# A hybrid attention and MLP block in fp32: gate sums spread over four up-projection units, and unused products on TensorE in three waits at the turn to the MLP

## The chip, the core and the metric

The kernel runs on one core of one Trainium2 chip. The metric is the device time of one execution in microseconds. A program on one core has one span; the median of several executions is compared.

## What is computed

One encoder block on 512 tokens of width 2048, in fp32. Two attention groups share an input projection and an output projection; their result is gated and added to x. Then comes the MLP, which is where the change lies:

```python
mod = c_act @ w_ada[l] + b_ada[l]
sh_a, sc_a, gt_a, sh_m, sc_m, gt_m = [m[:, None, :] for m in jnp.split(mod, N_MOD, axis=-1)]
...
o = o @ w_out[l]
x = x + gt_a * rms_norm(o, g_post_attn[l])

h = rms_norm(x, g_pre_mlp[l]) * (1.0 + sc_m) + sh_m
y = jnp.square(jax.nn.relu(h @ w_mlp_in[l])) @ w_mlp_out[l]
x = x + gt_m * rms_norm(y, g_post_mlp[l])
```

The hidden width is 8192. The gate of the MLP, gt_m, is a product of the activated vector c with 2048 columns of w_ada; it is wanted only at the very end, multiplied by g_post_mlp.

## The kernel before

Every engine has its own program, and they meet at semaphores. A matrix product in fp32 is done as three products of split values: an operand is split into a high part (`hi`, rounded, by ScalarE) and a low part (`lo`, the rest, by VectorE), and TensorE multiplies high by high, high by low and low by high, 128 x 128 weights against 512 columns each time.

**The turn to the MLP.** The last block of the output projection is done token tile by token tile (L2444 to L2446), so that VectorE can start on tile 0 early: it adds and gates a tile (L1739, L1744), adds it to x (L1790), and ScalarE sums squares and scales (L1104, L1087). The last of the four tiles is scaled by VectorE itself (L1810), for lack of time on ScalarE. TensorE, behind its last output product, waits for the last tile sum (`b_sum`), then turns the first 512 columns of each scaled tile, four transposes a tile, into banks 4 to 7 (L2462 to L2470), waiting for each tile (`xn_ready`). ScalarE and VectorE read the turned banks, scale and shift them (L1114, L1115, L1816), and split them into `h2_hi` and `h2_lo` (L1118, L1821). `first_columns` (L2474 on) is TensorE's first MLP unit, taken apart so that it can start with `h2_hi` of one row block alone (L2481, L2482: eight products), then take its `h2_lo` (L2485), then the second row block (L2489 to L2491). Bank 0 is free at the turn until L2481 writes it. `o_hi` is the high part of the old attention output; it lies where `h2_hi` will be written.

**The up-projection.** The MLP has eight groups of 1024 hidden columns. Each has two halves of eight units; a unit is 24 products (`unit_columns`, L2082 to L2084). The halves use banks 0 to 3 and 4 to 7 in turn. ScalarE and VectorE square the relu of a finished half, split it, mix it for the fast down product, and GpSimd stores it to DRAM (`y_dram`, L2698): a store waits for the one before it. Weights pass through a ring of four raw slots that SP fills.

**The gate.** Over groups 0 to 6, VectorE multiplies rows of w_ada by c and adds them up in `gm_acc` (L1262, L1265), 128 partial sums a column. In the last group TensorE adds the partitions: a product with a matrix of ones for each 512 columns (L2549), all four ahead of unit 6 of the first half, into banks 4 to 7, which the second half will use from unit 8 on. One count of `gm_reduced` is given by the last of them. ScalarE waits for it behind its work for unit 9 (L1168) and copies the four banks back into `gm_acc` (L1170), counting `gm_copied`. TensorE waits for four of these before unit 8 (L2553). GpSimd waits for four as well (L2714), then does four rounds in series: load 512 entries of b_ada and of g_post_mlp, spread to all partitions, into `rows` (L2711, L2712), add the one and multiply by the other (L2716, L2717). Then it gives `comb_m_ready`, and goes on to the four stores of the last group's activation.

**The down products.** SP, behind its last up loads, waits for `comb_m_ready`, because y values 1 lie where `rows` was, then issues the load of y values 1 and of weight blocks 22 and 21 for the first half of columns; behind TensorE's last up product the y values 2, 3 and 4; behind VectorE's last `y_ready` y values 6; behind all stores y values 5 and the blocks 11, 12 and 22 of the second half of columns. VectorE's down group (`dn_group`) begins with the difference of blocks 22 and 12 (L1893), then low halves (L1889) and further differences in a fixed order, with the last relu work of the up phase between them, and it takes finished banks away (L1963). TensorE's down unit is 12 products (L2519 to L2521); 14 such units make one half of columns.

The queue on each engine is fixed by the order in which the program is written. SP's loads, in short:

```python
sp.wait_ge(comb_m_ready, 1)
values(0, 1)
for k, (blk, h) in enumerate((("22", 0), ("22", 1), ("21", 0), ("21", 1))):
    sp.wait_ge(raw_used, MLP_RAW_END - RING + k + 1)
    weights(0, 0, blk, (h,))
sp.wait_ge(w_used, DN_W)
for k in (2, 3, 4):
    values(0, k)
sp.wait_ge(y_ready, GROUPS * PAIRS)
values(0, 6)
sp.wait_ge(y_saved, 16 * GROUPS * PAIRS)
values(0, 5)
weights(0, 1, "11")
```

Of the kernel before, what the change touches and what calls it, by code (L numbers as in the profile page):

```python
# [26 lines left out]
P = 128  # L27
T = 512
NT = T // P
D = 2048  # L30
KD = D // P
COLS = 512
NB = D // COLS
# [7 lines left out]
GROUPS = 8  # L41
FCH = D_FF // GROUPS // P
# [7 lines left out]
UNITS_D = KD // QROWS  # L50
# [143 lines left out]
def build(nc, a, out, x1_dram, y_dram):  # L194
    with ExitStack() as ctx:
# [22 lines left out]
        ones = small("ones", [P])  # L218
# [72 lines left out]
        gm_acc = sb("gm_acc", 180, [D])  # L291
# [426 lines left out]
        def _(act):  # L718
# [436 lines left out]
            def mlp_group(g, first=False, last=False):  # L1155
                for j in range(FIRST_SPLIT if first else 0, MLP_N):
                    r, w = at_mlp(g, j)
                    split_hi(r, w)
                    if 3 <= j < 6 and not first:
                        if j == 3:  # L1160
                            act.wait_ge(w_used, w.count(1, 1 - 4))
                        after_up(g - 1, 1, j - 3)
                    if UNITS_D + 3 <= j < UNITS_D + 6:
                        if j == UNITS_D + 3:
                            act.wait_ge(w_used, w.count(1, 1 - 4))
                        after_up(g, 0, j - UNITS_D - 3)
                    if last and j == UNITS_D + 1:
                        act.wait_ge(gm_reduced, 1)  # L1168
                        for n in range(NB):
                            nc.scalar.activation(gm_acc[:, n * COLS:(n + 1) * COLS], sets[1][n][:], ACT.Copy).then_inc(gm_copied, 1)  # L1170

# [883 lines left out]
        def _(pe):  # L2055
            mm = nc.tensor.matmul

            def unit_tokens(w, acc, act_hi, act_lo, k0, first, last, tiles=None, only=range(NT), behind_first=None):

                s = w.slot()  # L2060
                for t in only:
                    if t and tiles:
                        ins.then_inc(tiles, 1)
                    if t == 1 and behind_first:
                        behind_first()
                    for q in range(QROWS):
                        k = k0 + q
                        xh, xl = act_hi[:, k, t * P:(t + 1) * P], act_lo[:, k, t * P:(t + 1) * P]
                        mm(acc[t][:], xh, hi[s][:, q, :], start=first and q == 0, stop=False)  # L2069
                        mm(acc[t][:], xh, lo[s][:, q, :], start=False, stop=False)  # L2070
                        ins = mm(acc[t][:], xl, hi[s][:, q, :], start=False, stop=last and q == QROWS - 1)  # L2071
                if t == NT - 1:
                    ins.then_inc(w_used, 1)
# [387 lines left out]
            def turn_x1(k, t, out_bank):  # L2461
                return nc.tensor.transpose(out_bank[:, t * P:(t + 1) * P], z_tok[:, t, k * P:(k + 1) * P], ident[:])  # L2462

            pe.wait_ge(b_sum, 4 * NB)
            for t in range(NT):
                pe.wait_ge(xn_ready, t + 1)
                for k in range(4):
                    ins = turn_x1(k, t, bank[4 + k])
                    if t == NT - 1:
                        ins.then_inc(xn_turned, 1)  # L2470
            pe.wait_ge(row_done, 4 * NB)


# [69 lines left out]

            def spread_gm(j):

                if j == UNITS_D - 2:
                    pe.wait_ge(y_done, (GROUPS - 1) * FCH)
                    for n in range(NB):
                        ins = mm(sets[1][n][:], ones[:], gm_acc[:, n * COLS:(n + 1) * COLS], start=True, stop=True)  # L2549
                    ins.then_inc(gm_reduced, 1)  # L2550

            up_block(GROUPS - 1, 0, spread_gm)
            pe.wait_ge(gm_copied, NB)  # L2553
# [206 lines left out]
```

## Time and profile before

| | us |
|---|---|
| three runs | 2116.38, 2115.14, 2108.70 |
| their median | 2115.14 |
| the profiled execution, its own time | 2110.3 |
| its span, first to last instruction | 2108.6 |
| TensorE matmul busy | 2058.1 |
| VectorE busy | 1498.1 |
| ScalarE busy | 843.6 |
| GpSimd busy | 154.6 |
| mean granted TensorE clock | 0.993 |

The times of single instructions come from the profiled execution, in microseconds from its first instruction. Its span leaves out 1.7 us that its own time has around it. PE is TensorE, DVE VectorE, ACT ScalarE, POOL GpSimd, SP the engine that issues most transfers; L12 is line 12 of the kernel. Products overlap in their pipeline: the duration of one (0.39 us) is longer than the pitch from one to the next.

### The profile page before, as it was taken

What the parts mean: (1) busy time and instruction counts of PE and PEld (TensorE: products, weight loads), DVE (VectorE), ACT (ScalarE), POOL (GpSimd) and SP (SyncE); (2) the same over time, 40 slices, a digit from 0 to 9 for tenths busy, and PEclk for the clock granted to TensorE, in tenths of its full rate; (3) what the DMA queues carried; (4) which work ended last, traced back from release to release, by engine and by line L of the source; (5) the groups of instructions that cost most, each with busy time, mean ns of one, the idle gap of its engine ahead of it and who ended that gap; (6) DMA issues with size and microseconds to landing.
All of it is one profiled execution on the core that took longest, in us unless ns stands there. A gap on an engine that the chain in (4) does not pass through costs nothing.

```text
span 2108.6 us, 26190 instructions
## 1 busy us (share of the span) xinstructions
PE 2058.1 (98%) x9314; PEld 1701.0 (81%) x9314; DVE 1498.1 (71%) x1804; ACT 843.6 (40%) x1153; POOL 154.6 (7%) x163
## 2 busy tenths in 40 slices
PE   6999999999999989999999999999999999999998
PEld 6888888878888778888888888888788888888886
DVE  5986898788877766455444554435889888888866
ACT  4454223588833364233223333333333433333322
POOL 0000000157500000000000000012000000000000
PEclk9999999999999999999999999999999999999999
DMA  9997768600377637656665566676757356456442
GB/s 312 335 310 232 256 208 244 200 20 11 110 262 246 231 139 253 196 181 219 229 200 187 189 216 231 199 239 225 252 222 269 136 212 250 159 199 239 179 180 80
DMA packets 214353, 435.20 MB, mean 206 GB/s; under 512 B 30180, under 2 KB 69768, under 8 KB 205448
## 3 DMA queue, kind: packets, MB, share of 16 engines
q1 hardware_dynamic: 196136, 361.43, 51.0%
q0 software_dynamic: 16704, 67.11, 9.0%
q10 hardware_dynamic: 1440, 5.70, 0.7%
q8 instruction: 44, 0.72, 0.1%
q14 instruction: 29, 0.24, 0.0%
HBM read 367.09 MB, written 67.11 MB: 206 GB/s over the span
## 4 chain that ended last, share of the span: by engine, by line
PE 83%; DVE 6%; DMA 4%; ACT 3%; issue 3%; SPq 0%; DVEq 0%; ACTq 0%; POOLq 0%
PE bank L2082 11%; PE bank L2084 11%; PE bank L2083 11%; PE bank L2519 7%; PE bank L2520 7%; PE bank L2521 7%; PE bank L2069 5%; PE bank L2071 5%; PE bank L2070 5%; PE bank L2570 1%; PE bank L2569 1%; PE bank L2568 1%; DMA raw<-in_w_ada 1%; PE bank L2140 1%; DMA w<-in_w_mlp_out 1%
## 5 line engine op out<-in xcount | busy, mean ns | idle before, releaser
L1238 DVE TENSOR_TENSOR lo<-raw,hi 128x1024 fp32r<-128x1024 f32 (+2 forms) x234 | 276.4, 1185 | 373.7 <-ACT hi L725 371.5
L725 ACT ACTIVATE hi<-raw 128x1024 fp32r<-128x1024 f32 (+2 forms) x236 | 239.7, 1023 | 654.6 <-PE bank L2084 410.4
L2082 PE MATMUL bank<-h_hi,hi 128*128 128x512 f32 x1016 | 396.0, 390 | 0.0
L2084 PE MATMUL bank<-h_hi,lo 128*128 128x512 f32 x1016 | 395.3, 389 | 0.0
L2083 PE MATMUL bank<-h_lo,hi 128*128 128x512 f32 x1016 | 395.2, 389 | 0.0
L2519 PE MATMUL bank<-hi,y_use 128*128 128x512 f32 x784 | 307.7, 392 | 7.8 <-DVE acc L1965 3.8
L2520 PE MATMUL bank<-lo,y_use 128*128 128x512 f32 x784 | 306.1, 390 | 0.0
L2521 PE MATMUL bank<-hi,y_use 128*128 128x512 f32 x784 | 306.1, 390 | 0.0
L1181 ACT ACTIVATE hi<-w 128x1024 fp32r<-128x1024 f32 x168 | 178.3, 1062 | 296.8 <-PE bank L2521 218.3
L1889 DVE TENSOR_TENSOR lo<-w,hi 128x1024 fp32r<-128x1024 f32 x168 | 204.1, 1219 | 37.3 <-ACT hi L1181 36.2
L2082 PEld LDWEIGHTS bank<-h_hi,hi 128*128 128x128 f32 x1016 | 190.8, 188 | 40.0 <-issue 0.6
L2084 PEld LDWEIGHTS bank<-h_hi,lo 128*128 128x128 f32 x1016 | 190.7, 188 | 39.7
L2083 PEld LDWEIGHTS bank<-h_lo,hi 128*128 128x128 f32 x1016 | 190.8, 188 | 39.5 <-issue 0.2
L2519 PEld LDWEIGHTS bank<-hi,y_use 128*128 128x128 f32 x784 | 147.8, 189 | 43.6 <-issue 13.2
L2521 PEld LDWEIGHTS bank<-hi,y_use 128*128 128x128 f32 x784 | 147.8, 189 | 31.0
L2520 PEld LDWEIGHTS bank<-lo,y_use 128*128 128x128 f32 x784 | 147.9, 189 | 30.4
L2069 PE MATMUL bank<-hi,h_hi 128*128 128x512 f32 x320 | 125.9, 394 | 1.4 <-ACT q_o L883 1.4
L2071 PE MATMUL bank<-hi,h_lo 128*128 128x512 f32 x320 | 124.7, 390 | 0.0
L2070 PE MATMUL bank<-lo,h_hi 128*128 128x512 f32 x320 | 124.5, 389 | 0.0
L1965 DVE TENSOR_TENSOR acc<-bank,acc 128x1024 f32<-128x1024 f32 x84 | 102.1, 1216 | 0.0
L2069 PE MATMUL bank<-hi,o_hi 128*128 128x512 f32 x224 | 88.7, 396 | 0.1
L2071 PE MATMUL bank<-hi,o_lo 128*128 128x512 f32 x224 | 87.3, 390 | 0.0
(326 smaller groups left out, 3111.6 us busy)
## 6 DMA issues: line engine op xcount, KB each, us to landing
raw<-in_w_ada SPq DMA_DIRECT2D x192, 512.0 KB, 5.1
raw<-in_w_mlp_in SPq DMA_DIRECT2D x128, 512.0 KB, 4.3
w<-in_w_mlp_out SPq DMA_DIRECT2D x128, 512.0 KB, 5.2
y_dram<-y_out POOLq DMA_DIRECT2D x32, 1792.0 KB, 8.7
y_use<-y_dram SPq DMA_DIRECT2D x53, 1024.0 KB, 8.8
raw<-in_w_in SPq DMA_DIRECT2D x32, 512.0 KB, 5.6
raw<-in_w_out SPq DMA_DIRECT2D x32, 512.0 KB, 5.0
raw<-in_w_in SPq DMA_DIRECT2D x48, 256.0 KB, 5.5
```

The source lines that it names most:

```text
L725: ins = nc.scalar.activation(dst, src, ACT.Copy)
L1238: ins = tt(dst, src, high.bitcast(F32), ALU.subtract)
L1889: tt(lo[w.slot()][:], weight(np, i, h)[:], hi[w.slot()][:].bitcast(F32), ALU.subtract).then_inc(dn_lo, 1)
L2069: mm(acc[t][:], xh, hi[s][:, q, :], start=first and q == 0, stop=False)
L2070: mm(acc[t][:], xh, lo[s][:, q, :], start=False, stop=False)
L2071: ins = mm(acc[t][:], xl, hi[s][:, q, :], start=False, stop=last and q == QROWS - 1)
L2082: mm(acc[n][:], wh, act_hi[:, k, :], start=first and q == 0, stop=False)
L2083: mm(acc[n][:], wh, act_lo[:, k, :], start=False, stop=False)
L2084: ins = mm(acc[n][:], wl, act_hi[:, k, :], start=False, stop=last and q == QROWS - 1)
L2519: mm(bank[b + m][:], yh, hi[s][:, q, :], start=j == 0, stop=False)
L2520: mm(bank[b + m][:], yh, lo[s][:, q, :], start=False, stop=False)
L2521: ins = mm(bank[b + m][:], yl, hi[s][:, q, :], start=False, stop=j == PAIRS - 1)
```

## The change

Five places on TensorE, one on ScalarE. `gm_reduced` is now counted once per sum, so ScalarE waits for four.

```diff
@@ ScalarE, behind its work for unit 9 of the last group
-                        act.wait_ge(gm_reduced, 1)
+                        act.wait_ge(gm_reduced, NB)
                         for n in range(NB):
                             nc.scalar.activation(gm_acc[:, n * COLS:(n + 1) * COLS], sets[1][n][:], ACT.Copy).then_inc(gm_copied, 1)
@@ TensorE
             mm = nc.tensor.matmul
+
+            def keep_busy(n, out_bank, held, moving):
+
+                for _ in range(n):
+                    mm(out_bank, held, moving, start=True, stop=True)
@@ the turn to the MLP
+            keep_busy(4, bank[0][:], o_hi[:, KD - 1, 0:P], o_hi[:, KD - 1, :])
             pe.wait_ge(b_sum, 4 * NB)
             for t in range(NT):
+                if t == NT - 1:
+                    keep_busy(17, bank[0][:], o_hi[:, KD - 1, 0:P], o_hi[:, KD - 1, :])
                 pe.wait_ge(xn_ready, t + 1)
                 for k in range(4):
                     ins = turn_x1(k, t, bank[4 + k])
                     if t == NT - 1:
                         ins.then_inc(xn_turned, 1)
+            keep_busy(4, bank[0][:], o_hi[:, KD - 1, 0:P], o_hi[:, KD - 1, :])
             pe.wait_ge(row_done, 4 * NB)
@@ the last group, first half
             def spread_gm(j):
 
-                if j == UNITS_D - 2:
-                    pe.wait_ge(y_done, (GROUPS - 1) * FCH)
-                    for n in range(NB):
-                        ins = mm(sets[1][n][:], ones[:], gm_acc[:, n * COLS:(n + 1) * COLS], start=True, stop=True)
-                    ins.then_inc(gm_reduced, 1)
+                if j >= UNITS_D - NB:
+                    n = j - (UNITS_D - NB)
+                    pe.wait_ge(y_done, (GROUPS - 1) * FCH - NB + n + 1)
+                    mm(sets[1][n][:], ones[:], gm_acc[:, n * COLS:(n + 1) * COLS], start=True, stop=True).then_inc(gm_reduced, 1)
 
             up_block(GROUPS - 1, 0, spread_gm)
```

The 25 products of `keep_busy` multiply a part of the old `o_hi` with itself into bank 0; nothing reads what they write. UNITS_D is 8 and NB is 4, so the gate sums stand ahead of units 4, 5, 6 and 7.

## Rows read from the trace of the kernel before

**Rows 1.** The page, part 1: busy us, share of the span, instructions.
```profile
PE 2058.1 (98%) x9314; PEld 1701.0 (81%) x9314; DVE 1498.1 (71%) x1804; ACT 843.6 (40%) x1153; POOL 154.6 (7%) x163
```
**Rows 2.** TensorE's waits: line, releaser, us in total, times, longest.
```profile
PE bank L2462 <- DVE z_tok L1810: 3.9, 1, 3.9
```
**Rows 3.** Timeline of the turn: start us, us, engine, line, instruction [idle before <-releaser].
```profile
748.12 0.39 PE L2446 MATMUL bank<-hi,o_lo 128*128 128x512 f32 x1
...
749.56 1.06 PE L2462 MATMUL bank<-ident,z_tok 128*128 128x128 f32 x8 [1.05 <-DVE part L1739]
...
751.52 0.66 PE L2462 MATMUL bank<-ident,z_tok 128*128 128x128 f32 x4 [0.91 <-ACT z_tok L1087]
...
755.55 1.41 DVE L1810 TENSOR_SCALAR z_tok<-x_res,rstd 128x512 f32<-128x512 f32 x2
...
756.10 1.12 PE L2462 MATMUL bank<-ident,z_tok 128*128 128x128 f32 x4 [3.92 <-DVE z_tok L1810]
756.70 0.76 ACT L1114 ACTIVATE h_f<-bank,shf_m,gsc_m 128x512 f32<-128x512 f32 x1
...
758.15 1.29 DVE L1821 TENSOR_TENSOR h_lo<-h_f,h_hi 128x512 fp32r<-128x512 f32 x2 [0.47 <-ACT h_hi L1115]
...
758.27 0.77 PE L2481 MATMUL bank<-h_hi,hi 128*128 128x512 f32 x1 [1.05 <-ACT h_hi L1115]
...
761.50 1.09 PE L2485 MATMUL bank<-h_lo,hi 128*128 128x512 f32 x4
...
762.42 0.39 PE L2489 MATMUL bank<-h_hi,hi 128*128 128x512 f32 x1
```
**Rows 4.** TensorE in a stretch of the turn: stretch, length, busy, granted clock, DMA.
```profile
754.00:754.50 0.50, 0.00 (x0) 0.76 0.51 213
```
**Rows 5.** Timeline of the gate sums, TensorE and ScalarE.
```profile
1407.11 3.59 PE L2549 MATMUL bank<-gm_acc,ones 128*128 128x512 f32 x8
...
1410.74 2.07 ACT L1170 ACTIVATE gm_acc<-bank 128x512 f32<-128x512 f32 x4 [2.32 <-PE bank L2549]
1410.77 0.40 PE L2083 MATMUL bank<-h_lo,hi 128*128 128x512 f32 x1
```
**Rows 6.** Timeline of GpSimd's gate rounds: first add, a slow multiply, the last multiply.
```profile
1413.51 1.28 POOL L2716 TENSOR_TENSOR gm_acc<-gm_acc,rows 128x512 f32<-128x512 f32 x1 [10.47 <-DMA rows<-in_g_post_mlp]
...
1424.02 2.17 POOL L2717 TENSOR_TENSOR gm_acc<-gm_acc,rows 128x512 f32<-128x512 f32 x1
...
1443.58 1.30 POOL L2717 TENSOR_TENSOR gm_acc<-gm_acc,rows 128x512 f32<-128x512 f32 x1
```
**Rows 7.** SP from 1380 to 1530: a row of its waits, one of its timeline.
```profile
SPq L611 <- POOLq L2718: 19.5, 1, 19.5
...
1445.33 2.46 SPq L604 DMA_DIRECT2D w<-in_w_mlp_out  x4
```
**Rows 8.** Timeline of the first down units: VectorE, and TensorE's units 0 and 6.
```profile
1458.32 1.23 DVE L1893 TENSOR_TENSOR diff<-w,w 128x1024 f32<-128x1024 f32 x1 [12.36 <-DMA w<-in_w_mlp_out]
...
1478.32 2.35 DVE L1889 TENSOR_TENSOR lo<-w,hi 128x1024 fp32r<-128x1024 f32 x2
...
1464.95 0.39 PE L2519 MATMUL bank<-hi,y_use 128*128 128x512 f32 x1
...
1481.27 0.39 PE L2519 MATMUL bank<-hi,y_use 128*128 128x512 f32 x1
```
**Rows 9.** Timeline: GpSimd's stores 2 to 4, SP's next weights, TensorE's second wait.
```profile
1460.55 0.96 POOL L2698 DMA_DIRECT2D y_dram<-y_out  x1 [13.97 <-DMA y_dram<-y_out]
1473.74 0.94 POOL L2698 DMA_DIRECT2D y_dram<-y_out  x1 [12.23 <-DVE y_out L1852]
1481.89 0.94 POOL L2698 DMA_DIRECT2D y_dram<-y_out  x1 [7.21 <-DMA y_dram<-y_out]
...
1489.38 34.69 SPq L604 DMA_DIRECT2D w<-in_w_mlp_out  x14
...
1506.12 0.76 PE L2519 MATMUL bank<-hi,y_use 128*128 128x512 f32 x1 [2.92 <-DVE lo L1889]
```

## The prediction

> **What bounds the kernel now.** The page first: TensorE's matmuls fill 98% of the span [rows 1]. A change that adds or removes nothing large on TensorE can only act through the few stretches in which TensorE waits. The list of TensorE's waits names 3.9 us at the turn to the MLP, for the last normalised tile [rows 2]; in it stands also one of 2.9 us in the first group of down products, for a low half of a weight, whose own row is in rows 9. The timeline of the turn [rows 3] and the clock there [rows 4] price the first edit. For the second I followed the gate sums from TensorE to ScalarE's copies [rows 5], to GpSimd [rows 6], to the SP queue [rows 7], to VectorE's first down work [rows 8] and to the second wait [rows 9].
>
> **The products at the turn (25 added).** After its last output product, begun at 748.12 and streaming until about 748.35, TensorE waits until 749.56 for VectorE's tile, turns two tiles, waits 0.91 us, turns tile 2 (751.52, 0.66 us), waits 3.92 us and turns tile 3 at 756.10; then it waits for the first h2_hi until 758.27 [rows 3]. The granted clock (2.4 GHz) is full until about 754.2 (a mean of 0.76 over 754.0 to 754.5) [rows 4] and then half. At full clock products follow at 0.23 us ((762.42 - 761.50) / 4), at half clock at 0.40 ((761.50 - 758.27) / 8, the last of them already faster) [rows 3].
>
> - Four products ahead of the b_sum wait take 4 x 0.23 = 0.92 us, from 748.35 to 749.27. The wait ends at 749.56: cost nothing, hidden by 0.3 us of it.
> - Seventeen products behind the third tile's turn take 17 x 0.23 = 3.9 us from about 752.0 (751.52 plus four turns at some 0.11 us): they end at about 755.9, and tile 3 is ready at 756.1. Cost nothing, but the cover left is 0.2 us. From above: if the clock falls at 754.2 all the same, some 7 products still to come run at about 0.40 instead of 0.23 and the turn comes 1.0 us late. From below: nothing is gained by the products themselves.
> - Four products behind the fourth tile's turn, about 756.6 to 757.5, fit ahead of the first h2_hi.
>
> What they buy: with the clock held, the turn of a tile takes 0.66 instead of 1.12 us, and ScalarE, which starts 0.60 us behind the first of the half-clock turns [rows 3], starts about 0.3 us earlier; so does the first MLP product. The eight products from 758.27 to 761.50 take 8 x 0.23 = 1.84 instead of 3.23 us. The h2_lo tiles that the next products want are written by 759.44 [rows 3], so no new wait takes over at once. Together 0.3 + 1.4 = 1.7 us gained (bounds: 1.0 lost, 1.7 gained). I take the gain: the clock survived waits of 1.05 and 0.91 us here, fell only two microseconds into the long one [rows 3, 4], and the products leave no gap longer than the first two. All later MLP work is released by TensorE or behind it, so the gain should carry on.
>
> **The gate sums, on TensorE.** The eight passes (two per sum) run from 1407.11; the product that would have been at 1407.34 comes at 1410.77: 3.43 us for four sums, or 0.86 each [rows 5]. One ahead of each of units 4 to 7 costs the same 3.43 us. The bank waits are spread too, but VectorE released those banks long before unit 4. Cost: nothing; gain: nothing.
>
> **The gate sums, for those who wait.** Here the change has a price. ScalarE copies all four sums only when the count is 4 (before: 1, set by the last sum). It did so at 1410.74, done at 1412.81 [rows 5]. Now the last sum stands ahead of unit 7, that is one unit later, a unit being 24 products, 24 x 0.227 = 5.44 us (0.227 is (1481.27 - 1464.95) / 72 down products of the same shape [rows 8]). TensorE has by then done the same sums, so the copies start at 1410.74 + 5.44 = 1416.2 and end at 1418.25. Behind them on ScalarE stands the high half of unit 10, some 2 us late, wanted by TensorE 14 us later: hidden. TensorE itself wants the copies at unit 8 (about 1421.4): hidden.
>
> GpSimd is not hidden. Its first gate product started at 1413.51, released by the landing of its rows [rows 6], so 0.7 us of the delay is absorbed, and it now starts at about 1418.35: **4.85 us later**. Behind it are four rounds in series (two row loads, an add, a multiply), each released by the round before: 1413.51 to 1444.88. The whole series moves by 4.85 us. At its end SP waits: the row SPq L611 <- POOLq L2718 gives 19.5 us, and only then come the loads of y values 1 and of weights 22 and 21 [rows 7]. GpSimd's own next work, the four stores of the last activation, is behind the series as well; the third waits for VectorE and the fourth for the third [rows 9].
>
> VectorE was idle for 12.36 us until 1458.32, when weights 22 landed, and then works almost without a gap [rows 8]. It moves to about 1463.2. TensorE enters the down products at 1464.95 and takes a unit of 12 products in 2.72 us, so unit 6 is due at 1464.95 + 6 x 2.72 = 1481.27; its low half is done at 1478.32 + 1.2 = 1479.5 [rows 8]. The cover is 1.8 us, the smallest of the first units (unit 0, whose low half is done two instructions behind 1458.32, has 4.2), so TensorE first loses 4.85 - 1.8 = 3.05 us, in small waits. The 14 units after these hang on the stores: VectorE's y_out, store 3 (1473.74), store 4 when it has landed (1481.89), SP's loads behind store 4 (1489.38), weights 22 for the next half, VectorE, TensorE at 1506.12 after its 2.92 us wait [rows 9]. Every link is released by the one before, so TensorE resumes 4.85 us later than it did. The 3.05 us are part of that, not added to it. Nothing behind gives it back, TensorE being 98% busy.
>
> Bounds of this term: from below 0, if weights 22 did not really wait for their issue but for traffic that ends at a fixed time; from above 4.85 plus the slow form of GpSimd's multiply. In two of four rounds the multiply took 2.17 instead of 1.30 us [rows 6], when VectorE was reading; two more such rounds would give 6.6. I take 4.85, as all rows of the chain show release by the link before.
>
> The Trainium skill (GPSIMD Engine Reference, 8. Key points) says that GpSimd shares its SBUF interfaces with VectorE and contends with VectorE instructions that have two SBUF inputs. The trace's two multiply times agree with that. By the rule alone the moved rounds 2 and 3 meet VectorE again as before and round 4 not, which leaves 4.85; were all four to meet it, the term would be 6.6.
>
> **The sum.** -1.7 + 0 + 4.85 = **+3.1 us**. The profiled execution took 2110.3 us, so its like would take 2113.4; the median of the three runs shown is 2115.14, 4.8 above it, and 2115.1 + 3.1 = **2118.2 us**, which I forecast. What a measurement of this kernel can tell from no change is about 0.5%, 10.6 us: this is no change.
>
> **The rivals.**
> - *The gate chain is hidden.* The landing of weights 22 would be set by bandwidth (they took 13.0 us from 1445.33 to 1458.32 [rows 7, 8]), and later transfers with less beside them would catch up. Against it: SP's wait for GpSimd is plain. Then only the turn counts: 2115.1 - 1.7 = 2113.4. Chance 0.17.
> - *The clock falls at the turn all the same*, or the seventeen overrun: +1.0 instead of -1.7, with the gate chain +5.9: 2121.0. This is also the case in which the products do not do what they are for. Chance 0.12.
> - *Slower by over 0.5%: the stores pile up.* Store 2 would now start at about 1465.4, in the moment in which TensorE's end of the up phase releases three loads of y values. Stores are in series: each waits for the one before, and SP's loads for the last. Stores 3 and 4 took 8.2 and 7.5 us from issue to the next link (1473.74, 1481.89, 1489.38); the first held GpSimd for 14 us beside SP's loads [rows 9]. If 2, 3 and 4 each take 13, the last lands at 1465.4 + 39 = 1504.4 instead of 1489.4: +15.0, less 1.7, is +13.3: 2128.4. It decides once the three together take over 36 us (1465.4 + 36.3 is 12.3 late). Against it: GpSimd waited before store 3 for VectorE's y_out, not for store 2 [rows 9], so store 2 had room, and the added overlap is short. Chance 0.06.
> - *Faster by over 0.5%*: no row offers 10.6 us; only the scatter of the runs does. Chance 0.03.
>
> **How the numbers follow.** Forecast 0.62. The first three cases stay within 0.5%: 0.62 + 0.17 + 0.12 = 0.91 same, 0.06 slower, 0.03 faster. The range takes the runs' own scatter (2108.7 to 2116.4) with the terms: down to 2108.7 - 1.7 = 2107, up to 2116.4 + 6.6 + 1.0, and 2 for the start of the pile-up, 2126. It leaves out most of the slower case.
>
> **What would show it right or wrong.** In the changed profile: a clock of 1.00 from 748 to 764, ScalarE's first h_f some 0.3 us and the L2489 products about 1.7 us earlier against the last output product; four single gate sums with 0.86 us each; ScalarE's copies 5.4 us and SP's load behind GpSimd 4.9 us later against the start of unit 4; TensorE waits of about 3 us in all in the first half of the down products and a wait of about 4.7 in place of 2.9 at the second. If VectorE's first down work is not later by some 5 us, the gate term falls; if the clock still halves near 754, the turn term does. A second half-clock stretch in the first down products would break the claim that the small waits cost only themselves.

## The result, and the profile after

The changed kernel takes 2117.74 us (median of 12 runs, 2115.76 to 2126.38), the kernel before 2113.41 (12 runs, 2107.11 to 2116.38) in the same measurement. The medians are 4.3 us apart, the means (2118.50 and 2112.04) 6.5 us; the ratio over all runs is 1.003, with a 95% interval of 1.002 to 1.004, some 4 to 8 us. The slowdown is real, since 1.000 lies outside the interval, and smaller than the 0.5% under which the prediction speaks of no change. The profiled execution took 2115.81 us with a span of 2114.1, against 2110.3 and 2108.6 before: +5.5.

The page and the list of TensorE's waits (line, releaser, us in total, times, longest) of the changed kernel. The 25 products are there (9339 matmuls for 9314 in [rows 1]), and the busy time is 6.4 us more.

```profile
span 2114.1 us, 26240 instructions
...
PE 2064.5 (98%) x9339; PEld 1705.0 (81%) x9339; DVE 1498.7 (71%) x1804; ACT 843.5 (40%) x1153; POOL 154.1 (7%) x163
...
PE bank L2528 <- DVE lo L1889: 8.1, 4, 6.2
```

The last row is the one to look at: the wait of 2.9 us in the down products [rows 9] has become 8.1 us in four pieces, the longest 6.2.

The turn to the MLP, timeline of the changed kernel (L2467 was L2462, L2494 was L2485):

```profile
749.32 0.39 PE L2451 MATMUL bank<-hi,o_lo 128*128 128x512 f32 x1
...
752.72 0.66 PE L2467 MATMUL bank<-ident,z_tok 128*128 128x128 f32 x4 [1.08 <-ACT z_tok L1087]
753.13 4.13 PE L2061 MATMUL bank<-o_hi 128*128 128x512 f32 x17
...
757.31 0.66 PE L2467 MATMUL bank<-ident,z_tok 128*128 128x128 f32 x4
...
757.91 0.76 ACT L1114 ACTIVATE h_f<-bank,shf_m,gsc_m 128x512 f32<-128x512 f32 x1
...
759.48 0.47 PE L2490 MATMUL bank<-h_hi,hi 128*128 128x512 f32 x1 [0.58 <-ACT h_hi L1115]
...
761.39 1.07 PE L2494 MATMUL bank<-h_lo,hi 128*128 128x512 f32 x4
```

Stretches of the changed kernel (stretch, length, PE busy, granted clock, DMA share, GB/s), and under them one of the kernel before:

```profile
754.00:756.00 2.00, 2.00 (x11) 1.00 0.26 111
...
758.00:760.00 2.00, 1.42 (x6) 1.00 0.81 269
```
```profile
756.00:758.00 2.00, 1.12 (x4) 0.50 0.91 259
```

The clock is 1.00 (2.4 GHz) in every stretch of 2 us from 748 to 762; before it was 0.50 (1.2 GHz) from 756 to 760. The eight products that follow the first h_hi take 761.39 - 759.48 = 1.91 us, 3.23 before [rows 3]. ScalarE starts 0.60 us behind the last tile's turn, as before, although the turn now runs at full clock.

The gate chain, rows from the timelines of ScalarE, GpSimd, SP, VectorE and TensorE in the changed kernel:

```profile
1416.19 2.07 ACT L1170 ACTIVATE gm_acc<-bank 128x512 f32<-128x512 f32 x4 [6.09 <-PE bank L2558]
...
1418.41 1.29 POOL L2724 TENSOR_TENSOR gm_acc<-gm_acc,rows 128x512 f32<-128x512 f32 x1 [14.48 <-ACT gm_acc L1170]
...
1447.33 1.29 POOL L2725 TENSOR_TENSOR gm_acc<-gm_acc,rows 128x512 f32<-128x512 f32 x1
...
1449.08 2.50 SPq L604 DMA_DIRECT2D w<-in_w_mlp_out  x4
...
1463.17 1.22 DVE L1893 TENSOR_TENSOR diff<-w,w 128x1024 f32<-128x1024 f32 x1 [17.36 <-DMA w<-in_w_mlp_out]
...
1464.34 0.95 POOL L2706 DMA_DIRECT2D y_dram<-y_out  x1 [14.03 <-DMA y_dram<-y_out]
...
1479.70 0.94 POOL L2706 DMA_DIRECT2D y_dram<-y_out  x1 [14.41 <-DMA y_dram<-y_out]
...
1480.80 0.50 PE L2528 MATMUL bank<-hi,y_use 128*128 128x512 f32 x1 [0.59 <-DVE lo L1889]
...
1484.53 0.47 PE L2528 MATMUL bank<-hi,y_use 128*128 128x512 f32 x1 [0.72 <-DVE lo L1889]
...
1487.98 0.94 POOL L2706 DMA_DIRECT2D y_dram<-y_out  x1 [7.33 <-DMA y_dram<-y_out]
...
1496.20 33.98 SPq L604 DMA_DIRECT2D w<-in_w_mlp_out  x13
...
1512.78 0.77 PE L2528 MATMUL bank<-hi,y_use 128*128 128x512 f32 x1 [6.23 <-DVE lo L1889]
```

Read two releasers. GpSimd's first add is now released by ScalarE's copies, before by the landing of its rows [rows 6]. And store 3 (1479.70) is released by the landing of store 2; before it was VectorE's y_out [rows 9]. VectorE's y_out was itself 5.0 us later, counted from the turn (1477.61 against 1472.75), and store 2 held store 3 for another 1.1 us. The chain that ended last (start, us) shows how: stores 1 and 2 are on it whole, and store 2 takes twice what stores 3 and 4 take. It runs beside three loads of y values; before the change it had landed after 8.1 us.

```profile
1449.33 14.42 DMA y_dram<-y_out
...
1464.34 14.81 DMA y_dram<-y_out
...
1479.70 7.72 DMA y_dram<-y_out
1487.98 7.83 DMA y_dram<-y_out
```

**Where the time went.** Executions differ ahead of the change too: the last output product starts anywhere from 746.8 to 757.5 us in the profiles of this study. So I cut each profiled execution at three marks. A "turn" is one 128 x 128 transpose, and the first group of 16 turns of the MLP starts at 765.16 before and at 765.02 after. "Start" is the start of the last output product, A goes from it to the first group of 16 turns of the MLP, B from there to the end of TensorE's wait for the second half's first low half (of weights 22; 1506.12 before, 1512.78 after), C is the rest of the span. All in us.

| kernel | start | A | B | C |
|---|---|---|---|---|
| before | 748.12 | 17.04 | 740.96 | 602.48 |
| changed | 749.32 | 15.70 | 747.76 | 601.32 |
| turn_only | 748.19 | 15.70 | 739.99 | 601.32 |
| spread_only | 747.97 | 17.59 | 749.87 | 601.87 |
| one_earlier | 751.00 | 15.67 | 741.95 | 601.38 |
| weights_ahead | 749.55 | 15.73 | 749.87 | 602.25 |
| store_between | 757.52 | 15.72 | 751.83 | 601.43 |
| both_orders | 749.46 | 15.69 | 744.23 | 601.62 |
| both_and_earlier | 753.61 | 15.72 | 741.55 | 601.42 |
| seventeen_only | 749.69 | 15.68 | 749.43 | 601.70 |
| thirtyfour | 746.84 | 19.09 | 749.04 | 601.43 |
| eight_only | 747.21 | 16.25 | 748.65 | 601.59 |

The two kernels whose name begins with loads_ahead are not in the table, because their wait stands at another product. B and C together are 1350.03 for loads_ahead_changed and 1342.98 for loads_ahead_turn, against 1349.08 changed, 1341.31 turn_only and 1343.44 before.

Changed less before: +1.20 ahead of the change, -1.34 at the turn, +6.80 up to the second wait's end, -1.16 after it. The last three, which are the change's own, make +4.30; the medians say +4.33. That these agree so closely is luck: each column rests on one execution, and for spread_only and turn_only the same sum gives +8.85 and -3.47 where the medians say +7.0 and -4.4. Nor is the low clock at the turn a constant price: spread_only, with nothing changed at the turn, has an A that is 0.55 longer than before, so what the products save there is 1.3 to 1.9 us.

The -1.16 is clock: it is complete 36 products behind the wait, which are reached after 11.03 us before and after 9.88 in the changed kernel. Stretches around the second wait, before and then changed:

```profile
1504.00:1506.00 2.00, 0.00 (x0) 0.80 1.05 386
...
1512.00:1514.00 2.00, 2.00 (x10) 0.99 0.00 0
```
```profile
1508.00:1510.00 2.00, 0.00 (x0) 0.84 1.05 394
...
1516.00:1518.00 2.00, 2.00 (x10) 0.95 0.00 0
```

A mean of 0.80 over 2 us is 0.8 us at 0.50, so before the clock fell at about 1505.2; it was back at about 1512.0, after 6.8 us. By the same reading of the changed kernel it fell at about 1509.4 and was back at about 1516.2: 6.8 us too. But before only 0.9 us of them lay in the wait and 5.9 over products, and in the changed kernel 3.4 lay in the wait and 3.4 over products. A product takes 0.43 us at half clock and 0.227 at full, so 0.47 of such time is lost: 2.8 us before, 1.6 now, a difference of 1.2. The longer wait swallowed half of the low clock. Where the fall comes within a wait is no property of the change, so this part may differ from execution to execution: it came 2.0 us behind the start of the wait before, 2.8 us in the changed kernel and 4.8 us in one_earlier.

The marks of the gate chain, each counted from the first group of 16 turns, so that A and what lies ahead drop out:

| mark | before | changed | spread_only | one_earlier |
|---|---|---|---|---|
| GpSimd's first add | 648.35 | 653.39 | 653.46 | 648.28 |
| SP's loads of weights 22 | 680.17 | 684.06 | 685.78 | 679.60 |
| VectorE's first down work | 693.16 | 698.15 | 698.55 | 692.43 |
| store 2 | 695.39 | 699.32 | 701.04 | 694.80 |
| store 3 | 708.58 | 714.68 | 716.68 | 707.86 |
| SP's weights, second half | 724.22 | 731.18 | 733.32 | 725.45 |
| TensorE, end of second wait | 740.96 | 747.76 | 749.87 | 741.95 |

### The profile page after: what moved, and what is told of

It reads as the page before. It is cut to its first block, busy times and chain, and to the rows that moved or that the text cites. A ratio compares the mean times of both kernels' runs of the same rounds, so it can differ in the third digit from the quotient of the medians.

```text
span 2114.1 us, 26240 instructions
## 1 busy us (share of the span) xinstructions
PE 2064.5 (98%) x9339; PEld 1705.0 (81%) x9339; DVE 1498.7 (71%) x1804; ACT 843.5 (40%) x1153; POOL 154.1 (7%) x163
## 4 chain that ended last, share of the span: by engine, by line
PE 84%; DVE 5%; DMA 4%; issue 3%; ACT 3%; POOL 1%; SPq 0%; DVEq 0%; ACTq 0%; POOLq 0%
PE bank L2089 10%; PE bank L2087 10%; PE bank L2088 10%; PE bank L2528 7%; PE bank L2530 7%; PE bank L2529 7%; PE bank L2074 6%; PE bank L2076 6%; PE bank L2075 6%; DMA y_dram<-y_out 2%; PE bank L2578 1%; PE bank L2577 1%; PE bank L2576 1%; PE bank L2145 1%; PE bank L2146 1%
```

## The experiments

**First group: the parts alone, the place of the last sum, and SP's order.** The kernel before took 2112.49 us here (35 runs). The changed kernel was not measured again, here or in the two other groups; ratios are to the kernel before of the same group.

turn_only: the changed kernel with the gate sums and ScalarE's count as before.

```diff
-                        act.wait_ge(gm_reduced, NB)
+                        act.wait_ge(gm_reduced, 1)
@@ spread_gm
-                if j >= UNITS_D - NB:
-                    n = j - (UNITS_D - NB)
-                    pe.wait_ge(y_done, (GROUPS - 1) * FCH - NB + n + 1)
...
+                if j == UNITS_D - 2:
+                    pe.wait_ge(y_done, (GROUPS - 1) * FCH)
...
```

> The 25 products at the turn alone; the gate sums as before (four ahead of unit 6, one count). My theory: the clock stays full from 748 to 764, the eight L2490/L2491 products take 1.9 instead of 3.2 us, and nothing else moves: 1.3 to 1.7 us faster than the kernel before, and about 5 to 6 us faster than the changed one. Rival (the products overrun or buy nothing): 0 to 1 us slower than before.

Measured 2108.08 us (2106.19 to 2112.0), ratio 0.9981 (0.9969 to 0.9994): 4.4 us faster than before, where 1.3 to 1.7 had been expected. A is 1.34 shorter, B 0.97 and C 1.16. Timeline of the second wait:

```profile
1503.88 0.47 PE L2528 MATMUL bank<-hi,y_use 128*128 128x512 f32 x1 [1.95 <-DVE lo L1889]
```

The product behind the wait takes 0.47 us, not 0.76 as in [rows 9], and the granted clock is 1.00 in every stretch of 2 us from 1500 to 1522. What the 25 products do directly is A. B is a shorter second wait, 1.95 for 2.92 us, and C the half clock that did not come, 2.8 us, less a further wait of 1.09 us at 1510.69; that would be 1.7, and the 0.5 between it and 1.16 are not explained. The GpSimd multiplies took 1.28 to 1.30 us here, where two took 2.17 and 2.16 before [rows 6], but one add took 1.97 instead of 1.28. A single execution doesn't show that the turn causes this.

spread_only: the changed kernel without `keep_busy` and its three calls.

```diff
-            keep_busy(4, bank[0][:], o_hi[:, KD - 1, 0:P], o_hi[:, KD - 1, :])
-                    keep_busy(17, bank[0][:], o_hi[:, KD - 1, 0:P], o_hi[:, KD - 1, :])
-            keep_busy(4, bank[0][:], o_hi[:, KD - 1, 0:P], o_hi[:, KD - 1, :])
```

> The gate sums ahead of units 4 to 7 alone, ScalarE waiting for four; no products at the turn. My theory: GpSimd's first add starts about 4.9 us later, released by ScalarE's copy and no longer by its rows; TensorE's second down wait grows from 2.9 to 6 or 7 us; 5 to 7 us slower than before. Rival (the down phase is set by bandwidth, the gate chain hidden): within 0.5 us of before.

Measured 2119.45 us (2113.36 to 2125.65), ratio 1.0031 (1.0017 to 1.0045): +7.0. The two parts together are -4.4 + 7.0 = +2.6 by medians, where the whole change gave +4.3; the intervals of both parts reach some 3 us to either side, so they add up within what is measured. The expectation (5 to 7 us, a second wait of 6 or 7) held: 7.0, and 6.23. The delay stands in its column of the second table: 5.1 at the first add, 8.1 at store 3, 8.9 at TensorE.

one_earlier: the four single sums ahead of units 3, 4, 5 and 6, so that the last stands where all four stood before.

```diff
-                if j >= UNITS_D - NB:
-                    n = j - (UNITS_D - NB)
+                if UNITS_D - NB - 1 <= j < UNITS_D - 1:
+                    n = j - (UNITS_D - NB - 1)
```

> The changed kernel with the four gate sums ahead of units 3 to 6 in place of 4 to 7: still one per unit, but the last is where the four stood before. My theory (the price is the place of the last sum, not the spreading): GpSimd's first add goes back to being released by its rows, the second down wait back to about 2.9 us, and the time to that of turn_only, 5 us or so below the changed kernel. Rival (a lone fp32 sum between fp32r products costs TensorE or the clock something each time): it stays with the changed kernel.

Measured 2110.53 us (2107.09 to 2114.56), ratio 0.9989 (0.9976 to 1.0001). GpSimd's first add is again released by its rows:

```profile
1414.95 1.28 POOL L2724 TENSOR_TENSOR gm_acc<-gm_acc,rows 128x512 f32<-128x512 f32 x1 [9.19 <-DMA rows<-in_g_post_mlp]
```

All marks of its column are within 1.3 us of before. So the price hangs on the place of the last sum: one unit earlier it is gone. The expectation held only in part, though. The time was to be that of turn_only and is 2.45 us above it by medians (1.9 by means, 95% interval about 0.3 to 3.6), and the second wait is not back at 2.9:

```profile
1508.62 0.47 PE L2528 MATMUL bank<-hi,y_use 128*128 128x512 f32 x1 [3.73 <-DVE lo L1889]
```

A small cost of spreading as such, up to some 3 us, is therefore not ruled out.

weights_ahead: on SP, the loads of weights 22 and 21 ahead of the wait for the gate chain. If SP's wait is what carries the price, this takes it away.

```diff
-            sp.wait_ge(comb_m_ready, 1)
-            values(0, 1)
             for k, (blk, h) in enumerate((("22", 0), ("22", 1), ("21", 0), ("21", 1))):
...
+            sp.wait_ge(comb_m_ready, 1)
+            values(0, 1)
```

> The changed kernel with one order turned round on SP: the loads of weights 22 and 21 stand ahead of the wait for GpSimd's gate rounds, only y values 1 behind it. My theory (VectorE's late start hangs on that wait, the second TensorE wait on the stores behind the gate rounds): VectorE's first down difference no longer waits until 1463, the three small TensorE waits go, the stores have fewer loads beside them and take 8 instead of 15 us, and the second wait shrinks to under 3 us or goes: 7 to 10 us faster than the changed kernel, 3 to 5 faster than before. Rival (bandwidth decides, the bytes being the same): within 2 us of the changed kernel.

Measured 2117.58 us (2112.85 to 2122.86), ratio 1.002 (1.0006 to 1.0034). My expectation missed: VectorE no longer waits 17 us for its weights, and nothing is gained. Timeline of store 3 and of TensorE's last wait:

```profile
1480.97 0.94 POOL L2706 DMA_DIRECT2D y_dram<-y_out  x1 [14.76 <-DMA y_dram<-y_out]
...
1515.15 0.77 PE L2528 MATMUL bank<-hi,y_use 128*128 128x512 f32 x1 [6.13 <-DVE lo L1889]
```

Store 2 takes 15 us again and holds store 3. The prediction had two ways from GpSimd to the second wait, over SP and VectorE to y_out, and over the stores. This run cuts the first: y_out comes 1.1 us earlier than before, counted from the turn (1471.79 - 765.28 = 706.51, against 707.59), and store 3 still comes 7.1 us later. So the stores can carry the whole price alone. It does not show what the first way costs alone, and the edit has a price of its own: the weights now run beside the gate rounds, which end 3.4 us later than in the changed kernel (1450.99 - 765.28 = 685.71 against 682.31), and store 1 starts 4.3 us later.

**Second group: the stores' order.** Before: 2111.28 us (23 runs).

store_between: GpSimd issues the first store between gate rounds 2 and 3 instead of behind round 4.

```diff
+                if n == 1:
+                    save_pair(GROUPS - 1, 0, 0)
             pool.sem_inc(comb_m_ready, 1)
-            save_group(GROUPS - 1)
+            save_pair(GROUPS - 1, 0, 1)
+            save_pair(GROUPS - 1, 1, 0)
+            save_pair(GROUPS - 1, 1, 1)
```

> The changed kernel with one order turned round on GpSimd: the first store of the last activation (ready at 1430) stands between the second and the third gate round, not behind the fourth. SP's order is as in the changed kernel. My theory as the first four runs leave it (the second down wait hangs on the four stores in series behind the gate rounds; VectorE's late start costs only the small waits): stores 1 and 2 land some 10 us earlier, store 3 is again released by VectorE's y_out, the second wait falls from 6.2 to 3 to 5 us (VectorE being late still), the small first waits stay or grow to 2 to 3 us as SP's wait ends 1 to 2 us later; 1 to 3 us faster than the changed kernel. Rival (the landing of SP's own loads sets the second wait, not the stores): no change against the changed kernel.

Measured 2123.71 us (2120.2 to 2128.25, 6 runs), ratio 1.0057 (1.0038 to 1.0076): a miss, and the slowest of all. The store slows the row loads of round 3: the wait ahead of its add is 8.89 us, 3.66 in the changed kernel (round 4: 4.14 and 4.28). With the issue of the store and slower adds and multiplies, SP's wait ends 7.3 us later than in the changed kernel and VectorE gets its weights 4.5 us later, both counted from the turn. VectorE's row:

```profile
1475.84 1.22 DVE L1893 TENSOR_TENSOR diff<-w,w 128x1024 f32<-128x1024 f32 x1 [21.08 <-DMA w<-in_w_mlp_out]
```

TensorE waits 5.01 and 5.49 us, and behind both the first product takes 0.77 us, which is half clock. A store in the middle is paid by the rounds behind it.

both_orders: SP's order of weights_ahead and GpSimd's of store_between together.

```diff
@@ SP
-            sp.wait_ge(comb_m_ready, 1)
-            values(0, 1)
...
+            sp.wait_ge(comb_m_ready, 1)
+            values(0, 1)
@@ GpSimd
+                if n == 1:
+                    save_pair(GROUPS - 1, 0, 0)
```

> The changed kernel with both orders turned round: SP's weights 22 and 21 ahead of its wait for the gate rounds, and GpSimd's first store between rounds two and three. My theory: each alone leaves the other path in place; together nothing of the last stretch hangs on the gate rounds. VectorE's y_out for store 3 is then set by the end of the up products (1465), store 4 lands near 1486, and the second wait falls to between 0 and 2 us with no half clock: 2103 to 2107, 10 to 14 us below the changed kernel and 6 to 9 below before. Rival (bandwidth from 1440 to 1510 decides): the second wait stays at 5 us or more.

Measured 2112.75 us (2110.35 to 2118.69), ratio 1.0005 (0.9991 to 1.0019). Some 5 us better than the changed kernel in its own measurement, and as before, but the expectation of 2103 to 2107 missed and its rival, a second wait of 5 us or more, came. No small waits are left in the first down products, and store 3 stands at the place of before (1473.82 - 765.15 = 708.67 from the turn), but it is released by store 2, store 4 comes 11.8 us behind it (8.2 before), and the second wait is 6.03 us.

both_and_earlier: the same, with the sums at units 3 to 6.

```diff
@@ on top of both_orders
-                if j >= UNITS_D - NB:
+                if UNITS_D - NB - 1 <= j < UNITS_D - 1:
...
```

> As both_orders, and the gate sums ahead of units 3 to 6. My theory: with the gate rounds off the path, the place of the last sum no longer counts: within 1.5 us of both_orders. Rival (the place of the last sum has a price of its own on TensorE or ScalarE): 3 us or more faster than both_orders.

Measured 2109.46 us (2106.94 to 2113.97), ratio 0.999 (0.998 to 1.0001), the same as one_earlier. Against both_orders it is 3.3 us faster by medians (3.1 by means, 95% interval about 1 to 5), so the expectation of "within 1.5 us" missed: even with both orders turned round the place of the last sum still counts. The profiles say how: in both_orders the rounds end 2.6 us later (692.82 against 690.18 from the turn), store 2 starts 3.5 us later and takes 12.4 us, and store 3 waits for it. Timelines:

```profile
1476.81 0.96 POOL L2706 DMA_DIRECT2D y_dram<-y_out  x1 [14.32 <-DVE y_out L1852]
...
1510.88 0.47 PE L2528 MATMUL bank<-hi,y_use 128*128 128x512 f32 x1 [3.32 <-DVE lo L1889]
```

Here neither the stores nor the weights are late, and the second wait is still 3.3 us. What is left is a series that starts with the last up product: VectorE's y_out (7 us), stores 3 and 4 (8.3 and 9.4 us to the next link), SP's loads (some 14 to VectorE) and the low half (2.5), some 41 us, beside fourteen units of 2.72, 38.1 us. It comes out between some 40 us (turn_only, a wait of 1.95) and 42 us (one_earlier, 3.73), so about 2 to 4 us of wait are left, and in no run did an earlier end of the gate rounds bring it below 1.95.

seventeen_only: the changed kernel without the two calls with four products.

```diff
@@ ahead of the wait for b_sum
-            keep_busy(4, bank[0][:], o_hi[:, KD - 1, 0:P], o_hi[:, KD - 1, :])
@@ behind the fourth tile's turn
-            keep_busy(4, bank[0][:], o_hi[:, KD - 1, 0:P], o_hi[:, KD - 1, :])
```

> The changed kernel with the seventeen products alone, the two fours left out. Read at the turn alone: if the seventeen hold the clock by themselves, it is 1.00 from 748 to 766 and the first L2494 comes 12.1 us after the last output product as in the changed kernel (before: 13.4). If the fours are wanted too, the clock falls somewhere between 754 and 762.

One run, 2118.23 us, read at the turn only. The clock is 1.00 in every stretch of 2 us from 748 to 764, and A is 15.68 against 15.70: the seventeen alone hold the clock, and beside them the eight others buy nothing.

**Third group: the loads behind the stores, and the number of products.** Before: 2112.0 us (23 runs).

loads_ahead_changed: SP loads blocks 12 and 22 of the second half ahead of its wait for the stores; y values 5 and block 11 stay behind it. The first turn of SP's loop is written out for this.

```diff
-            sp.wait_ge(y_saved, 16 * GROUPS * PAIRS)
-            values(0, 5)
-            weights(0, 1, "11")
@@ dn_loads
                 weights(*to, "22", free=free(8))
+                if first:
+                    sp.wait_ge(y_saved, 16 * GROUPS * PAIRS)
+                    values(0, 5)
+                    weights(0, 1, "11")
```

> The changed kernel, but SP issues the blocks 12 and 22 of the second half of columns ahead of its wait for the stores, with only y values 5 and block 11 behind it (the loop's first turn is written out for that). My theory (four stores in series behind the gate rounds, then SP's 4 MB of loads, then VectorE, set the second down wait): VectorE's second down difference no longer comes 14 us behind the last store, the second wait of 6.2 us falls to 0 to 2, perhaps with a wait of 1 to 3 us for y values 5 instead; the small first waits stay. 4 to 7 us below the changed kernel. Rival (VectorE or bandwidth alone sets it): no change, or later stores.

Measured 2117.0 us (2114.23 to 2122.45), ratio 1.0029 (1.0016 to 1.0042). The expectation (4 to 7 us below the changed kernel) missed, and its rival, no change, came. The wait of 6.23 us for the low half is gone, and a wait for y values 5 is in its place. Timeline of that wait, and store 4 from the chain that ended last:

```profile
1504.70 0.79 PE L2531 MATMUL bank<-hi,y_use 128*128 128x512 f32 x1 [5.01 <-DMA y_use<-y_dram]
...
1486.77 13.04 DMA y_dram<-y_out
```

Store 4 takes 13.0 us instead of 7.8, because the weights now run beside it. The bytes are the same, and the DMA share in the changed kernel is 1.0 and more from 1504 to 1514 (1.05 at 394 GB/s in the row of 1508 above), so the order of the loads moves the wait and shortens it by 1.2 us, from 6.23 to 5.01. That gains nothing: from the turn to the end of the span this profile is 0.95 us longer than the changed kernel's.

loads_ahead_turn: the same edit on turn_only.

```diff
@@ on top of turn_only, SP's dn_loads
                 weights(*to, "22", free=free(8))
+                if first:
+                    sp.wait_ge(y_saved, 16 * GROUPS * PAIRS)
...
```

> The same SP order on turn_only (the 25 products, gate sums as before the change). If the last leg behind the stores is the floor under which no earlier gate round could bring the second wait, this is the kernel that goes below it: the wait of 2 to 3 us goes, and with it the half clock that sometimes follows: 2 to 5 us below turn_only, 5 to 8 below before. Rival: the loads collide with stores 3 and 4 and give the gain back: the time of turn_only.

Measured 2109.46 us (2104.59 to 2112.24), ratio 0.9987 (0.9975 to 0.9998), not told apart from turn_only: the rival again, where 2 to 5 us had been expected. The wait is 2.53 us, for y values 5 once more, and half clock follows it (0.58 over 1500 to 1502).

thirtyfour: 34 products in the middle call instead of 17.

```diff
-                    keep_busy(17, bank[0][:], o_hi[:, KD - 1, 0:P], o_hi[:, KD - 1, :])
+                    keep_busy(34, bank[0][:], o_hi[:, KD - 1, 0:P], o_hi[:, KD - 1, :])
```

> The changed kernel with 34 products in place of 17 behind the third tile's turn. Read at the turn: they end at 753.1 + 34 x 0.23 = 760.9 on the changed kernel's clock instead of 757.0, the last tile's turn comes 3.6 us late, and so do h_f and the first L2494, all at full clock. If the products yielded to work that becomes ready, there would be no delay.

One run, 2118.1 us. A is 19.09, 3.39 more than with 17. Timeline:

```profile
750.66 7.98 PE L2061 MATMUL bank<-o_hi 128*128 128x512 f32 x34
...
758.48 0.60 PE L2467 MATMUL bank<-ident,z_tok 128*128 128x128 f32 x4
```

The tile is turned only when the last product is through. It stands 11.64 us behind the last output product instead of 7.99, as expected. Once the cover is used up, each product too many costs its own 0.23 us.

eight_only: the seventeen out, the two calls with four kept.

```diff
-                if t == NT - 1:
-                    keep_busy(17, bank[0][:], o_hi[:, KD - 1, 0:P], o_hi[:, KD - 1, :])
```

> The changed kernel with the two fours and without the seventeen. Read at the turn: if the seventeen are what holds the clock, it falls to half near 754 to 756 after the last output product's time of 749 and the first L2494 comes 13.1 to 13.4 us behind the last output product, as before the change (12.07 with all 25); if the fours suffice, 12.1.

One run, 2115.35 us. A is 16.25, between 15.70 and the 17.04 of before, and the first L2492 (L2494 in the changed kernel) comes 12.62 us behind the last output product: neither the 13.1 to 13.4 nor the 12.1 that were expected. Timeline of the last turn, and the clock:

```profile
755.18 1.12 PE L2467 MATMUL bank<-ident,z_tok 128*128 128x128 f32 x4 [3.92 <-DVE z_tok L1810]
```
```profile
756.00:758.00 2.00, 2.00 (x7) 0.50 0.80 255
758.00:760.00 2.00, 2.00 (x10) 0.94 0.05 19
```

The clock falls during the wait of 3.92 us, as before. But the four products behind the last turn fill the time until the first h2_hi, and the clock is back at about 758.2, 11.0 us behind the last output product; before it was about 13.0. So with the seventeen the four are worth nothing, without them some 0.8 us of the 1.34, read from one execution.

## Why the prediction held, point by point

- **The forecast.** +3.1 us and 2118.2 us stand against +4.3 and 2117.7, and "no change by 0.5%" is right. The time is closer than the reasoning: 0.5 us off, because a base that was 1.7 too high (2115.14 from three runs, 2113.41 from twelve) made up for a difference that was 1.2 too small; on the base of twelve runs the same sum gives 2116.5. By means the difference is 6.5, twice the forecast. In the profiles the turn's gain was 0.4 us too large and the gate chain's price 0.8 too small (6.80 - 1.16 = 5.64 for 4.85); inside the latter stand two errors of opposite sign, +1.95 and -1.16.
- **The products at the turn: right in mechanism, 1.34 us for 1.7.** The clock held, the seventeen ended in time (the last tile's turn stands 7.99 us behind the last output product, 7.98 before), the eight products gained 1.32 us. The 0.3 us of head start for ScalarE failed: it starts 0.60 us behind the turn at either clock. With the two calls of four left out nothing changed (seventeen_only).
- **The gate sums on TensorE: zero, right.** Units with a sum between them are 6.34 us apart, without one 5.44: 0.90 each where the four in a row cost 0.86. The first down product stands 699.8 us behind the first 16 turns before, and 700.7 in the changed kernel, 0.52 of it a wait for a low half.
- **The first add: +4.85 forecast.** In the profiles it is 4.90 later as they stand, and 5.04 counted from the turn.
- **"The whole series moves by 4.85": wrong on the way, right at VectorE.** Counted from the turn the rounds ended only 3.9 us later. Of the 1.15 us made up, 0.5 lie in the adds and multiplies (one multiply took 2.15 and one 1.62 us where two took 2.17 and 2.16) and 0.65 in shorter waits for rows. But weights 22 then took 14.1 us to land instead of 13.0, and VectorE moved by 4.99: two misses that cancel. The Trainium skill (GPSIMD Engine Reference, 8. Key points) has GpSimd contend with VectorE instructions of two SBUF inputs; multiplies of 1.29 to 2.17 us on the same shape agree with that. The timelines, before and then changed, show more: VectorE pays as well.

```profile
1422.66 1.28 POOL L2716 TENSOR_TENSOR gm_acc<-gm_acc,rows 128x512 f32<-128x512 f32 x1 [5.09 <-DMA rows<-in_g_post_mlp]
1422.79 2.24 DVE L1238 TENSOR_TENSOR lo<-raw,hi 128x1024 fp32r<-128x1024 f32 x1 [4.21 <-ACT hi L725]
```
```profile
1438.98 1.29 POOL L2725 TENSOR_TENSOR gm_acc<-gm_acc,rows 128x512 f32<-128x512 f32 x1
1439.15 2.21 DVE L1238 TENSOR_TENSOR lo<-raw,hi 128x1024 fp32r<-128x1024 f32 x1 [2.42 <-ACT hi L725]
```

  Before, GpSimd's add started first and took its usual 1.28 us, VectorE's low half took 2.24 instead of 1.22, and the multiply behind it at 1424.02, started while VectorE was at work, took 2.17. In the changed kernel a multiply at 1438.98 met the same VectorE instruction, but started first: it took 1.29 and VectorE 2.21. In these rows the one that started first kept its time, and the other was longer by about what was left of the first. Which round meets VectorE changed from kernel to kernel, so it was no fixed property of round 2 or 3, as I had it.
- **Small waits: 3.05 us forecast, 1.83 found** (0.52 at the first down product, 0.59 and 0.72; of the first I expected none, although my own figures, 4.85 of delay against a cover of 4.2, leave 0.65). They are contained in the later wait, so the size mattered to nothing.
- **The stores: the step that failed.** The prediction said that stores 3 and 4 hang on VectorE's y_out and so come 4.85 late, and that "store 2 had room". It had 4.8 us of it (landed at about 1468.7, y_out written at 1473.5), enough for a start 3.9 us later but not for a slower store: before it took 8.1 us, now it ran beside three loads of y values for 14.8 us, and store 3 waited for it. Store 3 came 6.1 late, the second wait grew from 2.92 to 6.23 and TensorE resumed 6.8 later instead of 4.85. This is the "stores pile up" rival, given 0.06 for a price of +15: true in kind, with a price of about 1.1 at store 3 and 0.9 at SP's loads.
- **"Nothing behind gives it back": wrong by 1.2 us.** The low clock around the second wait lasts 6.8 us in both profiles, and more of it lies inside the longer wait. I had not priced the clock there, though the 0.76 us of the product behind the wait in [rows 9] shows that it was at half.
- **The rivals.** "The gate chain is hidden" is out: one_earlier takes the price away by the place of one sum alone. "The clock falls anyway" is out by the granted clock. "Faster by over 0.5%" did not come in any version.

In one sum: -1.34 + 6.80 - 1.16 = +4.3, for -1.7 + 4.85.

Of all kernels run, turn_only has the lowest ratio, 0.9981 (0.9969 to 0.9994) of before: it takes the gain of the turn and leaves the sums where they were. loads_ahead_turn (0.9987) isn't told apart from it.

What stays open: why turn_only gains 4.4 us by medians when the turn itself is worth 1.34. In its profile the other 2.1 lie in a second wait short enough to keep the clock (B and C). Whether the turn brings this regularly, or only that execution had faster gate rounds, isn't shown. Two other kernels with the products at the turn and the last sum in time gained less by medians, one_earlier 2.0 and loads_ahead_turn 2.5 us, and one GpSimd multiply or more took over 2.1 us in both. So a gain of 1.3 to 4.4 us is what these runs support. Also open is whether spreading the sums costs up to some 3 us where the last one is in time (one_earlier against turn_only).

## What to carry to other kernels

When a group of small operations is spread out, ask where its *last* one lands: whoever needs all of them waits for that one, and spreading by moving later delays a chain that starts there, even when the engine itself loses nothing. Follow such a chain through every queue that it feeds, and ask at each transfer what it will now run beside. Products that only keep the clock up pay if they end before the tile that they wait for; each one too many costs its full time.

## What the runs showed of the hardware

- The clock can fall in the middle of a wait or after its end. Behind 1.95 us (turn_only) it stayed at 1.00. Behind 3.32 us (both_and_earlier) and 3.73 us (one_earlier) the first product still took 0.47 us at full clock, and the clock then fell, to 0.50 over 1512 to 1514 and over 1510 to 1512, while TensorE was already busy. Behind 2.92 and 6.23 us it had fallen before the products came. So a first product at full clock is no proof that a wait cost only itself: look at the stretches behind it.
- Of two stores of the same size in the changed kernel, one took 7.7 us with little beside it (store 3) and one 14.8 us beside three loads of y values (store 2).
- GpSimd's add and multiply with two inputs take 1.28 to 1.30 us, and up to 2.28 (weights_ahead) beside VectorE work with two inputs; where GpSimd starts first, VectorE's low half takes 2.2 us instead of 1.22.
- ScalarE's start behind four turns is 0.60 us at both levels of TensorE's clock, although the turns take 0.66 us at one and 1.12 at the other.
